# A head's transposes put between the two tiles of the next head's first outputs, and its gating put ahead of that chunk's statistics

## The reference

```
def retention_chunk(q, k, v, s, log_gamma):
    ...
    scores = einsum('bhid,bhjd->bhij', q, k) * decay
    inner  = einsum('bhij,bhjv->bhiv', scores, v)
    cross  = einsum('bhid,bhdv->bhiv', q_dec, s)
    s_new  = exp(log_gamma * C) * s + einsum('bhjd,bhjv->bhdv', k_dec, v)
    return inner + cross, s_new
...
mu, var = mean and variance of o over the 512 values of a head
o = (o - mu) * rsqrt(var + EPS) * gn_ret
y_ret = einsum('blv,vd->bld', o * silu(z_r), w_branch_ret)
```

## Time and profile before

| | |
|---|---|
| median of 3 runs | 3080.58 us (3078.3 to 3082.46) |
| the profiled execution | 3080.77 us |
| its span | 3079.2 us |
| mean granted TensorE clock | 0.993 |
| PE busy | 2982.3 us, 97% |
| DVE busy | 1838.0 us, 60% |
| ACT busy | 1152.7 us, 37% |
| POOL busy | 712.7 us, 23% |

### The profile page before, as it was taken

One profiled execution on the slowest core, in us unless ns is written; L12 is line 12 of the kernel. 1 busy time (PEld: TensorE's weight loads), 2 busy tenths in 40 slices (PEclk: granted clock), 3 DMA queues, 4 the chain that ended last, 5 costly groups with the idle time before them and its releaser, 6 DMA issues.

```text
span 3079.2 us, 36009 instructions
## 1 busy us (share of the span) xinstructions
PE 2982.3 (97%) x13000; PEld 2297.0 (75%) x13000; DVE 1838.0 (60%) x2590; ACT 1152.7 (37%) x1892; POOL 712.7 (23%) x503
## 2 busy tenths in 40 slices
PE   7999999999999999999999999999999999999997
PEld 5888888888778888888887888788888888862222
DVE  8666666765454757566665675667567566754331
ACT  5434344445554434444433333333333332332110
POOL 5242535343332343443432000000000000001110
PEclk9999999999999999999999999999999999999999
DMA  4535354436543444534446556635644674559885
GB/s 134 204 123 186 128 186 143 175 131 187 195 155 125 158 168 149 175 141 158 159 155 265 206 176 249 259 109 193 262 179 161 238 272 141 196 188 329 305 310 189
DMA packets 297599, 582.06 MB, mean 189 GB/s; under 512 B 24840, under 2 KB 167688, under 8 KB 286255
## 3 DMA queue, kind: packets, MB, share of 16 engines
q1 hardware_dynamic: 292039, 562.73, 51.6%
q0 software_dynamic: 5392, 17.12, 1.5%
HBM read 410.63 MB, written 169.50 MB: 188 GB/s over the span
## 4 chain that ended last, share of the span: by engine, by line
PE 84%; DVE 7%; DMA 3%; issue 3%; ACT 2%; POOL 1%; SPq 0%; DVEq 0%; ACTq 0%; POOLq 0%
PE bank L1168 25%; PE bank L1170 24%; PE bank L1169 24%; PE bank L1463 7%; PE bank L1501 2%; DMA raw<-in_w_branch_pool 2%; PE bank L1216 1%; DVE z_in L2171 1%; DVE win_a L1899 1%; DVE wa_lo L1899 1%; DVE z_lo L1899 1%; PE bank L1494 1%; DVE c_out L1899 1%; DVE xs L1913 1%; DVE xa_lo L1899 0%
## 5 line engine op out<-in xcount | busy, mean ns | idle before, releaser
L1168 PE MATMUL bank<-xa_hi,wa_hi 128*128 128x512 f32 x2240 | 884.9, 395 | 12.4 <-DVE c_out L1899 8.1
L1170 PE MATMUL bank<-xa_hi,wa_lo 128*128 128x512 f32 x2240 | 874.7, 390 | 0.0
L1169 PE MATMUL bank<-xa_lo,wa_hi 128*128 128x512 f32 x2240 | 873.4, 390 | 0.0
L1168 PEld LDWEIGHTS bank<-xa_hi,wa_hi 128*128 128x128 f32 x2240 | 421.6, 188 | 100.6 <-issue 15.6
L1170 PEld LDWEIGHTS bank<-xa_hi,wa_lo 128*128 128x128 f32 x2240 | 421.1, 188 | 88.9
L1169 PEld LDWEIGHTS bank<-xa_lo,wa_hi 128*128 128x128 f32 x2240 | 421.9, 188 | 84.4
L1899 DVE TENSOR_TENSOR wa_lo<-w_raw,wa_hi 128x512 fp32r<-128x512 f32 x320 | 312.6, 979 | 191.9 <-ACT wa_hi L1599 190.8
L1899 DVE TENSOR_TENSOR wa_lo<-w_sum,wa_hi 128x512 fp32r<-128x512 f32 x240 | 195.2, 814 | 224.9 <-ACT wa_hi L1599 224.9
L1899 DVE TENSOR_TENSOR w_lo<-raw,w_hi 128x512 fp32r<-128x512 f32 (+1 forms) x288 | 180.4, 658 | 222.2 <-ACT w_hi L1707 222.1
L1599 ACT ACTIVATE wa_hi<-w_raw 128x512 fp32r<-128x512 f32 x320 | 200.8, 628 | 245.7 <-PE bank L1170 242.1
L1707 ACT ACTIVATE w_hi<-raw 128x512 fp32r<-128x512 f32 (+1 forms) x288 | 165.8, 603 | 273.5 <-PE bank L1170 102.0
(11 more groups left out here) (241 smaller groups left out, 4608.8 us busy)
## 6 DMA issues: line engine op xcount, KB each, us to landing
w_raw<-in_w_in SPq DMA_DIRECT2D x80, 1024.0 KB, 5.1
v_d<-turned SPq DMA_DIRECT2D x64, 512.0 KB, 3.2
qk_s<-qk_d SPq DMA_DIRECT2D x32, 1024.0 KB, 7.4
v_s<-v_d SPq DMA_DIRECT2D x32, 1024.0 KB, 11.0
raw<-in_w_branch_ret SPq DMA_DIRECT2D x128, 256.0 KB, 4.1
s_w<-in_w_in SPq DMA_DIRECT2D x64, 512.0 KB, 5.0
tabs<-in_c_rope SPq DMA_DIRECT2D x16, 1024.0 KB, 6.6
qk_d<-high SPq DMA_DIRECT2D x32, 512.0 KB, 4.5
```

The lines of the kernel that those rows point to most:

```text
L1168: pe.matmul(out, lh, rh, start=first, stop=False, skip_group_check=onto)
L1169: pe.matmul(out, lh, rl, start=False, stop=False, skip_group_check=onto)
L1170: return pe.matmul(out, ll, rh, start=False, stop=last, skip_group_check=onto)
```

## The change

`output` gets a third argument with the tiles that it is to make. On PE the 16 transposes of the earlier head now stand between tile 0 and tile 1 of output(hb, 0), where they stood behind tile 1. On DVE gate_og(hb-1) now stands ahead of statistics(hb, 0), where it stood behind. Both hold for heads 1, 2 and 3 of each of the four blocks: twelve places. Nothing is added or removed but PE's repeated waits ahead of tile 1, whose values are those of tile 0's. ACT's code is the same.

```diff
-            def output(hb, c):
+            def output(hb, c, tiles=range(2)):
...
-                for t in range(2):
+                for t in tiles:
...
                     update(hb, 0)
-                    output(hb, 0)
+                    output(hb, 0, (0,))
                     if h:
                         turn_og(hb - 1)
+                    output(hb, 0, (1,))
                     update(hb, 1)
...
                     new_state(hb, 0)
-                    statistics(hb, 0)
                     if h:
                         gate_og(hb - 1)
+                    statistics(hb, 0)
                     if b and h == 0:
                         out_variance(b - 1)
                     output_bias(hb, 0)
```

## The result

The change made the kernel slower: 3094.45 us (median of 17 runs) against 3081.84 us (17 runs), a ratio of 1.0042 with a 95% interval of 1.0032 to 1.0052, or +9.9 to +16.0 us. In the medians it is +12.6 us. The forecast was +11.6 us with a range of 3086 to 3099.

The account below looks back on a forecast made before the run. PE, busy 97% of the span, was taken as the bound, losing time in waits for z_in. Heads 2 and 3 +5.6, head 1 +8.9, first block -2.9 made +11.6 us: 3092.3 us, range 3086 to 3099.

Parts of the forecast that it names:

- The twelve places and their wait: Heads 1 to 3 of four blocks: PE waits for z_in ahead of the branch, losing 0.97 us a place, 11.6 in all.
- Blocks 2 to 4, heads 2 and 3: +0.94 each: Six places: og_hi stands behind st_hi on ACT, which waits for the delayed tile 1; 0.94 us longer each, +5.6 together.
- Head 1 of blocks 2 to 4: +2.95 each: Three places: transposes also wait 1.91 us for the earlier head's normalisation, plus 0.1 restart and 0.94; +8.9 together.
- The first block: -0.95 each: Three places: st_hi waits for the state only there, so the wait ahead of the branch goes wholly; -2.9 together.
- The cover: Nine places: normalisation comes some 3.5 us later, still some 6 us before its user output(hb, 1), so it costs nothing.
- The sum: Heads 2 and 3 +5.6, head 1 +8.9, first block -2.9: together +11.6 us, 3092.3 us.
- ACT as no obstacle (-5.6): Rival: og_hi made once z_in is there; twelve waits go, -11.6, head 1's normalisation costs +6.0; 3075.1 us, chance 0.05.
- Head 1 like its neighbours: Rival: at head 1 of blocks 2 to 4 the normalisation is earlier than read; +5.6, 3086.2 us, chance 0.06.
- The late statistics: Rival: statistics behind the gating too late for something taken as covered, 1 us at nine places; 3101 us, chance 0.06.
- The clock in head 1's idle stretches (0.22): Rival: TensorE's clock falls in the three new idle stretches, up to 1.7 us each, 5.1 more; 3097.4 us, chance 0.22.
- the third rival: Head 1 of blocks 2 to 4 costs no more than its neighbours; +5.6, 3086.2 us, chance 0.06.
- the first branch of the second: ACT is no obstacle at all twelve places, but head 1's transposes wait for the normalisation; -5.6, 3075.1 us, chance 0.05.

Follow-up runs that it names:

- ACT's other order: The change with ACT's copy og_hi put ahead of its copy st_hi, against the kernel before: 3075.5 us, -5.1 us, ratio 0.9980.
- The kernel with head 1 alone: Both parts of the change at head 1 of blocks 2 to 4 only, against the kernel before: +9.0 us in the medians, ratio 1.0030.
- one half: DVE's part alone (gating ahead of the statistics, PE's order as before), against the kernel before: -5.9 us, ratio 0.9971.
- heads 2 and 3 alone: Both parts of the change at heads 2 and 3 of blocks 2 to 4 only, against the kernel before: +4.7 us, ratio 1.0017.
- one program: PE's part alone (transposes between the tiles, DVE's statistics still ahead of the gating), against the kernel before: +35.2 us, ratio 1.0103; again, one run: +32.1 us.

## Why the prediction was right

**The twelve places and their wait.** Right. What bounded them was PE's wait for the fourth `z_in`.

**Blocks 2 to 4, heads 2 and 3: +0.94 each.** Right in mechanism and size. From branch to branch a head of the third block took 43.22 us and takes 44.18 (2241.36 to 2285.54): +0.96. That `st_hi` is what holds is shown by ACT's other order. The trace agrees with the rule of the Trainium skill that ScalarE is strict FIFO (TensorE: Matmul & The Clock Gate, section on the 16x 32x32 array): two `z_in` were ready 2.68 us before `st_hi` could start, and no `og_hi` passed it. Before the change this could not be seen.

**Head 1 of blocks 2 to 4: +2.95 each.** Right: from its first update to the branch 13.10 us before (2223.76 to 2236.86), 16.03 after (2225.33 to 2241.36), +2.93. The kernel with head 1 alone gives +9.4 in the trace, +9.0 less both, against +8.9.

**The first block: -0.95 each.** Right: head 1 to head 2 and head 2 to head 3 take 39.49 and 39.48 us, 0.97 less than before, and no wait is left.

**The cover.** Right. `og` started 1.44 us after the branch in the kernel before (2281.52 against 2280.08) and starts 3.97 us after it now (2289.51 against 2285.54): 2.53 later against the branch, which is itself 0.95 late; together that is the 3.5 of the forecast. PE has no new wait at output(hb, 1).

**The sum.** +11.6 forecast, +10.9 in the blocks of the trace (+11.3 less both), +12.6 in the medians. The trace's blocks, from one block's last branch to the next's, came out at +4.69, +5.10 and +4.20 where 4.83 was forecast. The differences are those of another wait, that of the pooling products for low weights: 0.30, 0.29 and 0.70 us before, 0.17, 0.55 and none after. I had it at nothing; in a block it gives or takes up to 0.7 us. The low clock behind the 5.07 us of idle is another term that I had at nothing: its cost varies by up to 1.6 us from profile to profile.

**The rivals.** ACT as no obstacle (-5.6): fallen with the trace, but nearly that (-5.1) came true once ACT's order was changed. Head 1 like its neighbours: fallen. The late statistics: fallen, since PE waits nowhere anew behind them. The clock in head 1's idle stretches (0.22): fallen for stretches of 1.8 us; its price of 1.7 us was near the 1.3 to 1.6 us measured at stretches of 2.45. Two readings of mine behind it were loose. The first matmul after 0.7 us of idle is 0.50 or 0.51 us long, not 0.47. And a first matmul of usual length says nothing of the clock: at 10 of the 12 falls it had 0.50 us, and the fall came behind it. My last split of the chances was off by a hundredth or two: the third rival and the first branch of the second make 0.11, not 0.09.

## What to carry to other kernels

When work is moved on two engines so that a chain starts earlier, walk the whole chain through every engine's order, the untouched ones included: here an idle engine (ACT, 37% busy) held the chain, because the instruction next in its order waited for the very work that had been pushed back. The same edit gained or lost with the order of two calls on a third engine. And split a change before judging it: one half was worth -6 us, the other turned it to +12. And before you read a difference of a us or two from two traces, see what differs between two profiles of one kernel: here it was the clock at the start of the blocks.

## What the runs showed of the hardware

- PE idle for 1.6 to 1.8 us, with full work on both sides, left the clock at 2.4 GHz in 24 of 24 stretches of the change's two profiles (and in all 15 of the three kernels with ACT's order changed, head 1 alone, and heads 2 and 3 alone). Idle for 2.45 us lowered it to 1.2 GHz at 12 of 24 places, not the same places in two executions of one program, and each fall cost 1.3 to 1.6 us. I had put 0.22 on the first and had not thought of the second.
- At 10 of the 12 falls PE had started again, and its matmuls slowed down only 0.6 to 1.6 us behind the first one; at the other two the first was already 0.80 instead of 0.50 us long. So the rows at the idle time itself often don't show the fall.
- After 3.8 to 6.5 us of idle ahead of update(1, 0) the clock was at 1.2 GHz in all eleven profiles, for 2.9 to 6.1 us of the work behind it.
